# Scaling the near branch's probabilities on GpSimd instead of ScalarE in a sparse attention

## The chip, the core and the metric

The kernel runs on one core of a Trainium2 chip. Its engines work side by side, each on its own list of instructions in the order of the list, and they wait for each other through semaphores: TensorE (PE in the profile, its weight loads PEld), VectorE (DVE), ScalarE (ACT), GpSimd (POOL) and SyncE (SP), which issues DMAs. The metric is the time of one execution on the device in microseconds (us). A measurement here is the median of three executions.

## What is computed

The whole program is a block with two token mixers and an expert layer, followed by a context network of two layers. All is float32 with 256 tokens of 1024 features. The change is in the sparse attention of the first mixer, which is, cut to the part that matters:

```python
s_s = jnp.einsum('bgrtd,bgtmd->bgrtm', qb, ks) - slopes * dist_s      # selected blocks
p_s = masked_softmax(s_s, dist_s >= 0)
s_w = jnp.einsum('bgrtd,bgsd->bgrts', qb, kw) - slopes * dist_w       # the near (window) branch
p_w = masked_softmax(s_w, valid_w)
o_s = jnp.einsum('bgrtm,bgtmd->bgrtd', p_s, vs)
o_w = jnp.einsum('bgrts,bgsd->bgrtd', p_w, vw)
return gb[..., 0:1] * o_c + gb[..., 1:2] * o_s + gb[..., 2:3] * o_w
```

There are 8 heads of width 64 over 256 tokens. With 256 tokens the selected blocks and the window both span all keys, so each of the two branches is a 256 by 256 masked softmax per head, with its own keys and values, and both are mixed by gates. A third branch works on 15 compressed blocks.

## The kernel before

The program is a chain of stages. Long stages of matmuls, whose weights stream from memory and are split into a high and a low part (the lines L326, L332 and L705 to L707 that fill the profile), alternate with shorter ones that compute attentions and routings. Each stage is a block with one function for each engine, and a barrier stands between two blocks. The sparse attention is one block: it begins at 105.8 us of the profiled span, and the next block, the output projection `w_out`, starts its matmuls at 170.05 us. The HGRN recurrence (`hg`) and the compressed branch (`compare`) are woven into the same block.

The attention goes over 8 steps, (2 query blocks) x (4 pairs of heads), `NS = 8`. A step `u` works on 128 queries and two heads, and its scores lie as 2 halves (heads) of 512 columns: columns 0 to 255 are the selected branch, columns 256 to 511 the near branch. Each engine runs a loop over `i`, written by hand; in round `i` different engines are at different steps.

- TensorE, round i: the scores of step i (L1420, waits for the biased scores of step i-1), then the turning of the probabilities of step i-2 (L1429, 8 transposes of 128 by 128 from `pr` into PSUM), then what `hg` and `compare` put into this round, then the products with the values of step i-3 (L1450). Before the transposes stand two waits: `nsa_scaled` and `nsa_win_scaled` must both have reached u+1.
- VectorE, round i: the bias of step i (L1550, out of PSUM into `sc`) and its maximum (L1555), then `hg` and `compare`, then for step i-1 the chain that makes the scales: `sums` clipped (L1562), reciprocal (L1564), times the gates into `coef` (L1566), and then the selected columns of `pr` times `coef` (L1570, two instructions of 128x256). L1562, L1564 and L1566 each add one to `nsa_link`, so `nsa_link` of 3u+3 says that the scales of step u stand. L1570 adds to `nsa_scaled`.
- ScalarE, round i: copies of the turned probabilities of step i-2 from PSUM (L1600, `pT`), the four exponentials of step i with their sums (L1610, waits for the maximum), and then for step i-1 the near columns of `pr` times `coef` (L1616, two instructions of 128x256, after a wait for `nsa_link` of 3u+3), which adds to `nsa_win_scaled`.

`pr` has three buffers, `u % 3`. GpSimd does nothing in this block. In the block behind it, it adds up squares for a norm (L435, `tensor_tensor` of 128x256).

The two waits of TensorE, and what ScalarE does for them:

```python
pe.wait_ge(nsa_scaled, u + 1)
pe.wait_ge(nsa_win_scaled, u + 1)
...
act.wait_ge(nsa_link, 3 * u + 3)
for half in range(2):
    ins = act.activation(pr[:, u % 3, half, T:2 * T], pr[:, u % 3, half, T:2 * T], ACT.Copy, scale=coef[:, u % 3, 2 * half + 1:2 * half + 2])
ins.then_inc(nsa_win_scaled, 1)
```

Of the kernel before, what the change touches and what calls it, by code (L numbers as in the profile page):

```python
# [24 lines left out]
ACT = mybir.ActivationFunctionType  # L25
ALU = mybir.AluOpType
# [5 lines left out]
T = 256  # L32
# [150 lines left out]
def build(nc, dr):  # L183

    ctx = ExitStack()
    with ctx:
        def sem(name):
            return ctx.enter_context(nc.semaphore(name))
# [114 lines left out]
        def loads(sp, upto):  # L303

            for g in range(next_load[0], min(upto, n_pieces)):
                if g >= RAW:

                    _, _, split, n = pieces[g - RAW]
                    if g - RAW in own_end:
                        sp.wait_ge(*own_end[g - RAW])  # L310
                    else:
                        sp.wait_ge(lo_done if split else raw_used, n + 1)
                src, w, _, _ = pieces[g]
                sp.dma_start(raw[:, g % RAW, 0:w], src).then_inc(raw_loaded[g % RAW], 16)
            next_load[0] = max(next_load[0], min(upto, n_pieces))
# [4 lines left out]
        def split_hi(act, g):  # L320

            _, w, _, n = pieces[g]
            piece_loaded(act, g)
            if n >= SPLIT:
                act.wait_ge(piece_used, n - SPLIT + 1)
            act.activation(whi[:, n % SPLIT, 0:w], raw[:, g % RAW, 0:w], ACT.Copy).then_inc(hi_done, 1)  # L326
# [955 lines left out]
        NS = len(STEPS)  # L1282
        HALVES = [slice(0, 64), slice(64, 128)]
        nsa_scored, nsa_biased, nsa_max, nsa_exp = (sem(n) for n in ("nsa_scored_or_weighted_act", "nsa_biased_or_weighted_dve", "nsa_max_or_tokens_turned", "nsa_exp"))
        nsa_link, nsa_scaled, nsa_win_scaled = (sem(n) for n in ("nsa_link", "nsa_scaled", "nsa_win_scaled"))
# [7 lines left out]
        with ExitStack() as own, nc.Block() as block:  # L1293
            def ob(name, shape):
                return own.enter_context(nc.sbuf_tensor(name, shape, F32))
# [4 lines left out]
            pr = ob("nsa_pr", [P, 3, 2, 512])  # L1300
            nm, sums, coef = ob("nsa_nm", [P, 2, 4]), ob("nsa_sums", [P, 3, 4]), ob("nsa_coef", [P, 3, 4])
# [21 lines left out]
            def turn_bank(o):  # L1323
                return 2 + at_use[o] % 2
# [9 lines left out]
            @block.sync  # L1334
            def _(sp):
                loads(sp, at_wout + RAW)
# [244 lines left out]
            @block.scalar  # L1581
            def _(act):
                def block_done(qb):
                    bank = ps[:, 4 + qb, :]
                    act.wait_ge(block_attended, qb + 1)
                    act.activation(mixT[:, 4:8, qb * P:qb * P + P], bank.rearrange("p (c t) -> p c t", t=P), ACT.Copy).then_inc(block_out, 1)
                    act.activation(nsq[:, qb, :], bank, ACT.Square).then_inc(block_out, 1)

                def root(qb):
                    act.wait_ge(block_summed, qb + 1)  # L1590
                    act.activation(nroot[:, qb, :], ps[:, 4 + qb, 0:8], ACT.Sqrt, bias=eps[:, :], scale=1.0 / 64).then_inc(block_root, 1)

                for i in range(NS + 3):
                    if 0 <= i - 2 < NS:
                        u = i - 2
                        if u >= 2:
                            act.wait_ge(nsa_attended, u - 1)
                        for half in range(2):
                            act.wait_ge(nsa_turned, at_use[(u, half)] + 1)
                            act.activation(pT[:, u % 2, 512 * half:512 * half + 512], ps[:, turn_bank((u, half)), :], ACT.Copy).then_inc(nsa_copied, 1)  # L1600
                        if u == 2:
                            act.wait_ge(nsa_turned, at_use[("cmp", 0)] + 1)
                            act.activation(cT[:, :, :, :].rearrange("p h b t -> p (h b t)"), ps[:, turn_bank(("cmp", 0)), :], ACT.Copy).then_inc(nsa_copied, 1)
                    if i < NS:
                        act.wait_ge(nsa_max, i + 1)
                        if i >= 3:
                            act.wait_ge(nsa_turned, at_use[(i - 3, 1)] + 1)
                        for n in range(4):
                            half, a = divmod(n, 2)
                            act.activation(pr[:, i % 3, half, a * T:a * T + T], sc[:, i % 2, half, a * T:a * T + T], ACT.Exp, bias=nm[:, i % 2, n:n + 1],  # L1610
                                           accum_out=sums[:, i % 3, n:n + 1]).then_inc(nsa_exp, 1)
                    if 0 <= i - 1 < NS:
                        u = i - 1
                        act.wait_ge(nsa_link, 3 * u + 3)
                        for half in range(2):
                            ins = act.activation(pr[:, u % 3, half, T:2 * T], pr[:, u % 3, half, T:2 * T], ACT.Copy, scale=coef[:, u % 3, 2 * half + 1:2 * half + 2])  # L1616
                        ins.then_inc(nsa_win_scaled, 1)
                    if i == 2:
                        for b in range(TB):
                            act.wait_ge(hg_turned, b + 1)  # L1620
                            act.activation(kiT[:, b, :], ps[:, 6 + b, :], ACT.Copy).then_inc(hg_copied, 1)
                        act.wait_ge(cmp_link, 4)
                        act.activation(cs[:, :, :, :].rearrange("p h u n -> p (h u n)"), cs[:, :, :, :].rearrange("p h u n -> p (h u n)"), ACT.Exp).then_inc(cmp_exp, 1)
                    if i in (6, 7):
                        b = i - 6
                        act.wait_ge(hg_out, b + 1)
                        act.activation(osq[:, b, :], ps[:, 7 - b, :], ACT.Square).then_inc(hg_squared, 1)
                    if i == 7:
                        block_done(0)
                    if i == 8:  # L1630
                        act.wait_ge(hg_summed, 2)
                        act.activation(hsum[:, :, :], hsum[:, :, :], ACT.Sqrt, bias=eps[:, :], scale=1.0 / P).then_inc(hg_root, 1)
                    if i == 9:
                        root(0)
                block_done(1)
                root(1)

# [1623 lines left out]
```

## Time and profile before

| | |
|---|---|
| median of 3 runs | 2073.28 us (2072.81 to 2073.97) |
| the profiled execution | 2074.13 us |
| its span, first to last instruction | 2072.4 us |
| PE busy | 2004.6 us, 97% of the span |
| VectorE, ScalarE, GpSimd busy | 1458.1, 1063.0, 34.4 us |
| block of the sparse attention | about 105.8 to 169 us of the span |

Times in rows are us from the start of the span. A row of the timeline gives the start, the time until the end of the last of a run of like instructions, engine, line, operation, what is written and read, shape and count, and in brackets how long the engine had been idle before, with what ended it. "issue" there means that the profile shows nothing the engine waited for at that moment; a semaphore that came earlier, or a weight load, may stand behind it. In the table by stretches, PEclk is the mean granted clock of TensorE, 1.00 for 2.4 GHz and 0.50 for 1.2 GHz.

### The profile page before, as it was taken

Reading aid. Unit: us, or ns where it says so; the run is one execution under the profiler, and the core shown is the slowest. Engines: PE = TensorE matmul, PEld = TensorE weight load, DVE = VectorE, ACT = ScalarE, POOL = GpSimd, SP = SyncE. Lnnn points to the kernel's source line nnn. Section 1 sums busy time; section 2 is a strip of 40 time slices with the busy share of each in tenths; the row PEclk is TensorE's granted clock in tenths of the full one; section 3 lists DMA queues with packets and bytes.
Section 4 is the critical chain, followed back from the end, with each engine's and each line's share of the span. In section 5 each row is a group of like instructions: output and inputs, shape, how many; then the busy total and the mean of one; then the engine's idle time right before and its main releaser. Section 6 shows DMA issues by size and latency. Waiting matters only on the chain. (4 is left out here: it accounts for less than half of the span.)

```text
span 2072.4 us, 33517 instructions
## 1 busy us (share of the span) xinstructions
PE 2004.6 (97%) x13458; PEld 1765.5 (85%) x13458; DVE 1458.1 (70%) x2213; ACT 1063.0 (51%) x1979; POOL 34.4 (2%) x33
## 2 busy tenths in 40 slices
PE   8978999999999999999989999999999999999998
PEld 7858999999999888888787877878778888778998
DVE  7776599988888678888588657577774227667554
ACT  5674444467777555445573247453222227555444
POOL 0000000000000000000010000100000001000000
PEclk9988999999999999999999999999999999999999
DMA  6603566654444678777546520245674323125654
GB/s 224 206 1 122 164 191 185 192 168 139 143 133 143 198 245 267 250 257 259 162 135 200 171 67 22 92 133 173 232 272 136 100 94 98 42 69 157 194 188 127
DMA packets 95401, 328.98 MB, mean 159 GB/s; under 512 B 10384, under 2 KB 15888, under 8 KB 95248
## 3 DMA queue, kind: packets, MB, share of 16 engines
q1 hardware_dynamic: 95248, 326.85, 48.8%
q8 instruction: 107, 1.75, 0.3%
q14 instruction: 46, 0.38, 0.1%
HBM read 325.76 MB, written 1.05 MB: 158 GB/s over the span
## 5 line engine op out<-in xcount | busy, mean ns | idle before, releaser
L332 DVE TENSOR_TENSOR wlo<-raw,whi 128x1024 fp32r<-128x1024 f32 (+1 forms) x502 | 613.4, 1224 | 333.7 <-ACT whi L326 330.5
L326 ACT ACTIVATE whi<-raw 128x1024 fp32r<-128x1024 f32 (+1 forms) x502 | 525.5, 1049 | 380.9 <-PE ps L707 363.3
L705 PE MATMUL ps<-x_hi,whi 128*128 128x512 f32 (+1 forms) x976 | 333.5, 342 | 10.9 <-DVE x_lo L508 6.7
L706 PE MATMUL ps<-x_lo,whi 128*128 128x512 f32 (+1 forms) x976 | 329.9, 338 | 0.0
L707 PE MATMUL ps<-x_hi,wlo 128*128 128x512 f32 (+1 forms) x976 | 329.8, 338 | 0.0
L705 PE MATMUL ps<-xT_hi,whi 128*128 128x256 f32 x1136 | 324.1, 285 | 3.2 <-DVE xT_lo L506 2.8
L707 PE MATMUL ps<-xT_hi,wlo 128*128 128x256 f32 x1136 | 318.0, 280 | 0.0
L706 PE MATMUL ps<-xT_lo,whi 128*128 128x256 f32 x1136 | 317.9, 280 | 0.0
L705 PEld LDWEIGHTS ps<-x_hi,whi 128*128 128x128 f32 x976 | 184.1, 189 | 42.8 <-issue 13.6
L705 PEld LDWEIGHTS ps<-xT_hi,whi 128*128 128x128 f32 x1136 | 214.5, 189 | 3.5 <-issue 3.5
L706 PEld LDWEIGHTS ps<-xT_lo,whi 128*128 128x128 f32 x1136 | 214.5, 189 | 0.0
L707 PEld LDWEIGHTS ps<-xT_hi,wlo 128*128 128x128 f32 x1136 | 214.2, 189 | 0.0
L707 PEld LDWEIGHTS ps<-x_hi,wlo 128*128 128x128 f32 x976 | 184.3, 189 | 20.2
L706 PEld LDWEIGHTS ps<-x_lo,whi 128*128 128x128 f32 x976 | 184.3, 189 | 19.5 <-issue 0.2
L705 PE MATMUL ps<-whi,gh 128*128 128x512 f32 x512 | 200.1, 391 | 0.5 <-issue 0.5
L706 PE MATMUL ps<-wlo,gh 128*128 128x512 f32 x512 | 199.3, 389 | 0.0
L707 PE MATMUL ps<-whi,gl 128*128 128x512 f32 x512 | 199.3, 389 | 0.0
L1921 ACT ACTIVATE gh<-gated 128x256 fp32r<-128x256 f32 x128 | 53.4, 418 | 165.2 <-PE ps L707 165.2
L705 PE MATMUL ps<-ffn_hi,whi 128*128 128x512 f32 (+2 forms) x384 | 126.7, 330 | 0.9 <-DVE wlo L332 0.9
L707 PE MATMUL ps<-ffn_hi,wlo 128*128 128x512 f32 (+2 forms) x384 | 126.6, 330 | 0.0
L706 PE MATMUL ps<-ffn_lo,whi 128*128 128x512 f32 (+2 forms) x384 | 126.6, 330 | 0.0
L705 PEld LDWEIGHTS ps<-whi,gh 128*128 128x128 f32 x512 | 96.1, 188 | 22.6 <-issue 1.7
(431 smaller groups left out, 3331.8 us busy)
## 6 DMA issues: line engine op xcount, KB each, us to landing
raw<-peer_u_t SPq DMA_DIRECT2D x128, 512.0 KB, 3.6
raw<-peer_v_t SPq DMA_DIRECT2D x128, 512.0 KB, 4.0
raw<-ffn_in_t SPq DMA_DIRECT2D x88, 512.0 KB, 4.4
x<-ada_t SPq DMA_DIRECT2D x64, 512.0 KB, 4.5
raw<-ffn_out_t SPq DMA_DIRECT2D x44, 512.0 KB, 3.6
raw<-qkv_t SPq DMA_DIRECT2D x36, 512.0 KB, 4.2
gated<-ada_t SPq DMA_DIRECT2D x32, 512.0 KB, 5.9
raw<-w_in_t SPq DMA_DIRECT2D x24, 512.0 KB, 4.4
```

Source lines behind the costliest of these rows:

```text
L326: act.activation(whi[:, n % SPLIT, 0:w], raw[:, g % RAW, 0:w], ACT.Copy).then_inc(hi_done, 1)
L332: dve.tensor_tensor(wlo[:, n % SPLIT, 0:w], raw[:, g % RAW, 0:w], whi[:, n % SPLIT, 0:w].bitcast(F32), ALU.subtract).then_inc(lo_done, 1)
L705: pe.matmul(place, wh, xh, start=start, stop=False, skip_group_check=shared)
L706: pe.matmul(place, wh, xl, start=False, stop=False, skip_group_check=shared)
L707: return pe.matmul(place, wl, xh, start=False, stop=stop, skip_group_check=shared)
L1921: act.activation(gh[:, i % 3, :], gbuf[:, i, :], ACT.Copy).then_inc(gates_hi, 1)
```

## The change

The two ScalarE instructions at the end of each round are taken out, with their wait. GpSimd gets a function in this block: for each of the 8 steps it waits for the same `nsa_link` and multiplies the same columns with `tensor_scalar`, two instructions of 128x256, the second of which adds to `nsa_win_scaled`. TensorE and VectorE keep their instructions and waits.

```diff
                     if 0 <= i - 1 < NS:
                         u = i - 1
-                        act.wait_ge(nsa_link, 3 * u + 3)
-                        for half in range(2):
-                            ins = act.activation(pr[:, u % 3, half, T:2 * T], pr[:, u % 3, half, T:2 * T], ACT.Copy, scale=coef[:, u % 3, 2 * half + 1:2 * half + 2])
-                        ins.then_inc(nsa_win_scaled, 1)
+                        pass
...
+            @block.gpsimd
+            def _(pool):
+                for u in range(NS):
+                        pool.wait_ge(nsa_link, 3 * u + 3)
+                        for half in range(2):
+                            ins = pool.tensor_scalar(pr[:, u % 3, half, T:2 * T], pr[:, u % 3, half, T:2 * T], coef[:, u % 3, 2 * half + 1:2 * half + 2], None, ALU.mult)
+                        ins.then_inc(nsa_win_scaled, 1)
```

ScalarE's list in rounds 1 and 2 of the loop; `nsa_pr` are the probabilities, `nsa_coef` the scales, L1610 the exponentials, L1600 the copies of turned probabilities:

```order
 L1610 ACTIVATE nsa_pr,nsa_sums<-nsa_sc,nsa_nm 128x256 [waits nsa_max_or_tokens_turned]
 L1610 ACTIVATE nsa_pr,nsa_sums<-nsa_sc,nsa_nm 128x256 x3
-L1616 ACTIVATE nsa_pr<-nsa_pr,nsa_coef 128x256 [waits nsa_link]
-L1616 ACTIVATE nsa_pr<-nsa_pr,nsa_coef 128x256
 L1600 ACTIVATE nsa_pT<-ps 128x512 [waits nsa_turned] x2
```

Behind the exponentials of a step the copies of the step before now come at once; the wait for `nsa_link` is gone from ScalarE.

GpSimd's list at the start of the program and of the block; "ISA" is the instruction that the trace calls MODIFY_POOL_CONFIG:

```order
+L3254 MEMSET const-uint8-127 128x1
+L1635 UNCONDITIONAL_BRANCH [waits barrier_Pool_Activation_PE_DVE_SP_gather]
+L1640 ISA
+L1640 TENSOR_SCALAR nsa_pr<-nsa_pr,nsa_coef 128x256 [waits nsa_link]
+L1640 TENSOR_SCALAR nsa_pr<-nsa_pr,nsa_coef 128x256
```

The pair of L1640 stands there eight times. GpSimd's list where the next block begins, with the additions for the norm:

```order
+L1293 UNCONDITIONAL_BRANCH
 L844 UNCONDITIONAL_BRANCH [waits barrier_Pool_Activation_PE_DVE_SP_gather]
-L435 ISA
 L435 TENSOR_TENSOR x_ffn<-x_ffn 128x256 [waits early_squares]
 L435 TENSOR_TENSOR x_ffn<-x_ffn 128x256 [waits folded,early_squares] x3
```

The configuration has moved from the beginning of that block to the beginning of the attention's.

## Rows read from the trace of the kernel before

**Rows 1.** The page: span and busy time of the engines.

```profile
span 2072.4 us, 33517 instructions
...
PE 2004.6 (97%) x13458; PEld 1765.5 (85%) x13458; DVE 1458.1 (70%) x2213; ACT 1063.0 (51%) x1979; POOL 34.4 (2%) x33
```

**Rows 2.** One stretch: us long, busy by engine, PEclk, DMA share, GB/s.

```profile
150.00:160.00 10.00, 8.44 (x46) 7.81 (x47) 3.60 (x12) 7.70 (x18) 0.00 (x0) 0.54 0.00 0
```

**Rows 3.** Timeline of PE: the transposes of steps 0 to 4 and 6.

```profile
117.34 1.94 PE L1429 MATMUL ps<-kon,nsa_pr 128*128 128x128 f32 x8 [2.99 <-ACT nsa_pr L1616]
...
122.77 1.06 PE L1429 MATMUL ps<-kon,nsa_pr 128*128 128x128 f32 x8 [1.12 <-issue]
...
127.74 1.06 PE L1429 MATMUL ps<-kon,nsa_pr 128*128 128x128 f32 x8 [0.19 <-issue]
...
134.03 1.09 PE L1429 MATMUL ps<-kon,nsa_pr 128*128 128x128 f32 x8
...
139.69 1.06 PE L1429 MATMUL ps<-kon,nsa_pr 128*128 128x128 f32 x8 [0.73 <-issue]
...
151.56 1.94 PE L1429 MATMUL ps<-kon,nsa_pr 128*128 128x128 f32 x8 [3.55 <-issue]
```

**Rows 4.** Timeline of ACT: the near columns scaled, steps 0, 1, 2, 4, 6.

```profile
116.30 0.89 ACT L1616 ACTIVATE nsa_pr<-nsa_pr,nsa_coef 128x256 f32<-128x256 f32 x2
...
121.77 0.89 ACT L1616 ACTIVATE nsa_pr<-nsa_pr,nsa_coef 128x256 f32<-128x256 f32 x2
...
126.74 0.90 ACT L1616 ACTIVATE nsa_pr<-nsa_pr,nsa_coef 128x256 f32<-128x256 f32 x2
...
138.70 0.89 ACT L1616 ACTIVATE nsa_pr<-nsa_pr,nsa_coef 128x256 f32<-128x256 f32 x2
...
150.57 0.89 ACT L1616 ACTIVATE nsa_pr<-nsa_pr,nsa_coef 128x256 f32<-128x256 f32 x2
```

**Rows 5.** Timeline of DVE: the scales of steps 0 to 4, 6.

```profile
115.82 0.16 DVE L1566 TENSOR_TENSOR nsa_coef<-nsa_coef,gates 128x4 f32<-128x4 f32 x1
...
120.60 0.16 DVE L1566 TENSOR_TENSOR nsa_coef<-nsa_coef,gates 128x4 f32<-128x4 f32 x1
120.80 0.62 DVE L1570 TENSOR_SCALAR nsa_pr<-nsa_pr,nsa_coef 128x256 f32<-128x256 f32 x2
121.69 1.28 DVE L1550 SCALAR_TENSOR_TENSOR nsa_sc<-mkon,ps 128x512 f32<-128x512 f32 x2 [0.28 <-PE ps L1420]
...
126.47 0.17 DVE L1566 TENSOR_TENSOR nsa_coef<-nsa_coef,gates 128x4 f32<-128x4 f32 x1
...
132.30 0.16 DVE L1566 TENSOR_TENSOR nsa_coef<-nsa_coef,gates 128x4 f32<-128x4 f32 x1
...
138.04 0.16 DVE L1566 TENSOR_TENSOR nsa_coef<-nsa_coef,gates 128x4 f32<-128x4 f32 x1
...
149.47 0.17 DVE L1566 TENSOR_TENSOR nsa_coef<-nsa_coef,gates 128x4 f32<-128x4 f32 x1
```

**Rows 6.** PE and DVE where they wait for each other, 127 to 131 us.

```profile
130.88 1.13 PE L1367 MATMUL ps<-hg_v,sig 64*128 64x128 f32 x8 [1.11 <-DVE S L1478]
...
127.60 1.28 DVE L1550 SCALAR_TENSOR_TENSOR nsa_sc<-mkon,ps 128x512 f32<-128x512 f32 x2 [0.32 <-PE ps L1420]
```

**Rows 7.** GpSimd's line L435: ns shortest/median/longest, first and last start, forms.

```profile
L435 POOL TENSOR_TENSOR x<-x x24: 726/1292/2088, 1057.7 to 2063.9; 128x512 f32<-128x512 f32 x15, 128x256 f32<-128x256 f32 x9
L435 POOL TENSOR_TENSOR x_ffn<-x_ffn x4: 736/739/1587, 184.9 to 194.0; 128x256 f32<-128x256 f32 x4
L435 POOLq MODIFY_POOL_CONFIG  x2: 11/11/11, 169.0 to 169.0; - x2
```

**Rows 8.** Timeline, 2059 to 2066 us: GpSimd's additions beside DVE's tensor_scalar.

```profile
2060.21 2.51 POOL L435 TENSOR_TENSOR x<-x 128x256 f32<-128x256 f32 x3 [189.81 <-ACT x L425]
...
2061.11 0.88 DVE L2562 TENSOR_SCALAR final_weighted<-h,vec 128x256 f32<-128x256 f32 x1
...
2062.80 0.35 DVE L2562 TENSOR_SCALAR final_weighted<-h,vec 128x256 f32<-128x256 f32 x1
```

## The prediction

> **What bounds the kernel now.** I read the busy times first. TensorE is busy 2004.6 of the span's 2072.4 us, ScalarE half of it, GpSimd 2% [rows 1]. So nearly everywhere the time is matmuls, and an edit pays only where TensorE stands still. The block of the sparse attention is such a place: about 63 us in which all engines pass small pieces to one another. The blocks behind it are filled by matmuls without gaps, and nothing there has slack that depends on when it starts, so I carry a shift of this block's end one to one to the end of the program.
>
> Second, the timeline of TensorE within the block. Before the transposes (L1429) it stood idle for 2.99, 1.12, 0.19, 0.73 and 3.55 us at steps 0, 1, 2, 4 and 6, and not at all at step 3 [rows 3]. These are the places where the scaled probabilities came last; the row of step 0 names ScalarE's L1616.
>
> Third, who is late there. The scales of a step stand when VectorE's L1566 ends [rows 5]. From there to the end of ScalarE's two instructions [rows 4] it took: step 0, 117.19 less 115.98, 1.21 us; step 1, 122.66 less 120.76, 1.90; step 2, 127.64 less 126.64, 1.00; step 4, 139.59 less 138.20, 1.39; step 6, 151.46 less 149.64, 1.82. The two instructions themselves take 0.89 to 0.90 us; the rest is ScalarE still at the exponentials of the next step. TensorE starts 0.10 to 0.15 us after ScalarE's end (117.34, 122.77, 127.74, 139.69, 151.56) [rows 3]. So L1616 does end last at these five places, though VectorE's share (0.62 us for its own two [rows 5]) would be ready 0.3 to 1.2 us earlier.
>
> **What the change takes away.** ScalarE loses 16 instructions, 8 x 0.89 = 7.1 us of busy time. That is worth nothing by itself: ScalarE's exponentials wait for maxima or follow copies that wait for the transposes, so what it saves turns into waiting. The most that the change could bring is the near columns ready no later than VectorE's own: 0.04 + 0.62 us after the scales. Then TensorE would start earlier by 1.21 - 0.66 = 0.55 at step 0, 1.24 at step 1, 0.34 at step 2, 0.73 at step 4, 1.16 at step 6. These do not add up, because VectorE has its own chain. The gains of steps 0 to 2 end in TensorE's wait of 1.11 us for VectorE at 130.88, and VectorE itself can only close its own idle 0.28 and 0.32 us [rows 5, 6]: 0.6. Step 6 adds 1.16. That is the ceiling: about 1.8 us, under 0.1%.
>
> **What GpSimd costs.** The trace of before has no `tensor_scalar` on GpSimd. The nearest row is its `tensor_tensor` of the same 128x256: median 739 ns, 1587 at the longest [rows 7]. At 128x512 the median is 1292 ns, so 553 ns for 256 columns and 186 ns that do not depend on them. An instruction with one input instead of two might halve the 553: 186 + 277 = 0.46 us, my lower bound; 1.59 us is the upper. I take 0.74, the row of the same shape on the same engine.
>
> Then the port. VectorE's `tensor_scalar` of 128x256 takes 0.35 us alone, but 0.88 where it began while one of GpSimd's additions was running [rows 8], about as long as that addition's 0.74 and a little. So the two shut each other out. In the changed kernel they meet in every step: VectorE's L1570 and GpSimd's pair are released by the same semaphore. VectorE is a little ahead, since its own instruction set the semaphore. I let GpSimd wait for one of the two, 0.35 us. From the end of L1566 to GpSimd's end, which I call p: 0.1 for the semaphore + 0.35 + 2 x 0.74 = 1.93 us. Bounds: 0.1 + 2 x 0.46 = 1.0 without a wait, and 0.1 + 0.35 + 2 x 1.59 = 3.6.
>
> The Trainium skill (SBUF — State Buffer, section "Who interferes with whom") says that VectorE's `tensor_scalar` can enter a mode that takes the port pair it shares with GpSimd, and that the one that comes second waits for the whole instruction. The 0.88 above agrees. The skill's GPSIMD Engine Reference (section "When to use GPSIMD") speaks against the change in general: elementwise work belongs on VectorE, though one-input operations run at roughly line rate. By that rate p would be near its lower bound.
>
> **The sum, step by step.** GpSimd's end against ScalarE's end, each counted from the scales:
> - Step 0: 1.93 - 1.21 = +0.72. The transposes and what follows on TensorE, the scores for VectorE's L1550 at 121.69 included, come 0.7 later; VectorE was waiting for them (0.28 idle), so its whole list moves by 0.7.
> - Step 1: the scales come from VectorE's list before that, unmoved; 1.93 - 1.90 = +0.03.
> - Step 2: the scales are 0.7 late, and +0.93 on top: the transposes at +1.6. TensorE then has 1.11 us of waiting at 130.88 to give, so +0.5 is left; VectorE, with 0.32 idle at 127.60, is at +0.4 [rows 6]. Both go on at +0.5.
> - Step 3: TensorE came at 134.03 without a wait. The scales end at 132.46 + 0.5, GpSimd at 134.89, TensorE starts 0.15 later: 135.04, +1.0.
> - Step 4: the scales at +0.5, and 1.93 - 1.39 = +0.54: +1.0. TensorE itself is there at 1.0 - 0.73 = +0.3, so it waits for GpSimd.
> - From there TensorE works without a gap past step 5 to the scores of step 7, and VectorE follows them: the scales of step 6 at +1.0, and 1.93 - 1.82 = +0.11 more.
> - Behind step 6 TensorE is busy to the end of the attention, at half clock (151.56: the eight transposes take 1.94 us instead of 1.06 [rows 3]; mean granted clock 0.54 [rows 2]). Step 7's columns are ready before it gets to them.
>
> Sum: +1.1 us. The profiled execution took 2074.13 us, its span 2072.4 and 1.7 around it, so it would become 2075.2. The median of the runs is 0.85 below that execution; I forecast 2073.28 + 1.1 = 2074.4.
>
> GpSimd's other work costs nothing: its list in this block is otherwise empty, and the configuration that moved here is issued at about 105.9, ten us ahead of its first instruction, which waits for 115.98. No DMA moves, and SP's list is as before.
>
> **The rivals.** A measurement here can tell about 0.2% from no change, 4.1 us.
>
> 1. Cheap GpSimd: one input costs 0.46 us and the port does not bite, p = 1.0. Then step 0 is 0.2 early, step 1 0.9, step 2 unchanged, step 4 0.4 early, step 6 0.8; carried as above that leaves about 0.9 us gained: 2072.4. For it speaks the single input; against it the 0.88 of rows 8.
>
> 2. Dear GpSimd, the rival on the slower side: `tensor_scalar` with its scale read for each partition costs as much as the slowest rows of L435. At p = 3.6 the excess at step 0 is 2.4, at step 2 2.6, at step 4 2.2, at step 6 1.8, and TensorE's idle times (1.12, 1.11, 0.73) swallow only part: some 6.5 us, 2079.8. Between 0.74 (+1.1) and 1.59 (+6.5) it decides at 0.74 + 0.85 x 3.0 / 5.4, about 1.2 us for one instruction. Against it: the long rows of L435 stand beside two-input work on VectorE; alone it is 0.73 to 0.74 each time.
>
> 3. The configuration isn't hidden: something that follows MODIFY_POOL_CONFIG delays the first GpSimd instruction. Before, 15.9 us lay between it and the first addition (169.0 to 184.9), which took no longer than others [rows 7]; now 10.1 us lie there. The trace bounds a delay at 15.9 - 10.1 = 5.8 us, paid once, at step 0, and 4.5 after the idle times of steps 1 and 2: 2078.9 with the forecast's own 1.1.
>
> The Trainium skill (GPSIMD Engine Reference, section "Instruction dispatch") gives about 6 us for a first call after such a load; if that began only with the first call, it would be this rival, if it began with the configuration it would be hidden. No run here shows which.
>
> 4. The clock: TensorE fell to half clock after standing still for 2.99 and 3.55 us, not after 1.12 [rows 3]. With p = 1.93 it would stand for some 1.8 us before step 2. If that is enough, the groups after it take up to twice as long: 0.9 us for each set of eight transposes, some 1.8 us in all, 2076.2. Losing the low stretch behind 151.56 instead would gain 2 or 3 us, but the idle time before it does not get shorter.
>
> **How the numbers follow.** Forecast (p about 1.5 to 2.5) 0.62; cheap GpSimd 0.17; clock 0.08; dear GpSimd 0.08; configuration 0.05. Predicted 2074.4. The range goes down to the ceiling of the gain, 2073.28 - 1.8 = 2071.5, and up to where p is 2.9 or the clock falls once more, 2077.3; it leaves out most of rivals 2 and 3. Faster by over 0.2% would need more than twice the ceiling: 0.02. Slower by over 0.2%: rival 3 and most of rival 2, 0.11. The same: 0.87.
>
> **What would show it.** GpSimd's L1640 near 0.74 us each and its second one ending about 1.9 us behind L1566; VectorE's L1570 stretched from 0.62 towards 1.4 us where GpSimd got in between; TensorE's idle time before L1429 at step 2 grown from 0.2 to over 1 us; ScalarE 7 us less busy and waiting more; the next block's first matmul near 171.2 instead of 170.05. The forecast is wrong if L1640 takes over 1.2 us or under 0.5, if the first L1640 starts well after its semaphore, or if the low clock covers another stretch than before.

## The result

The changed kernel takes 2079.84 us (median of 20 runs, 2074.51 to 2082.09), the kernel before beside it 2074.74 us (20 runs, 2071.58 to 2076.50): the ratio is 1.0025 with a 95% interval of 1.0019 to 1.0031, 5.1 us slower. Forecast were 1.1 us. The profiled execution took 2079.41 us.

The page of the changed kernel, to be set beside [rows 1]: TensorE's busy time and GpSimd's have grown, ScalarE's has shrunk.

```profile
span 2077.6 us, 33517 instructions
...
PE 2008.0 (97%) x13458; PEld 1768.3 (85%) x13458; DVE 1460.0 (70%) x2213; ACT 1058.7 (51%) x1963; POOL 50.4 (2%) x49
```

The time went into the block of the sparse attention. In this profile the block's first scores began 0.69 us later than before (106.61 against 105.92 us; the mean clock over the program's first 50 us is 0.93 here and 1.00 there, and the change doesn't touch them), and the first matmul of the next block came at 175.33 instead of 170.05. So the block itself took 5.28 - 0.69 = 4.6 us longer, and all behind it as long as before (1904.1 us in both).

The timeline of the changed kernel's TensorE: the transposes of steps 0 to 4 and 6, which answer to [rows 3], and the scores of step 3.

```profile
119.60 1.94 PE L1429 MATMUL ps<-kon,nsa_pr 128*128 128x128 f32 x8 [3.87 <-POOL nsa_pr L1640]
...
123.18 2.08 PE L1420 MATMUL ps<-nqk 64*128 64x512 f32 x4
125.19 1.10 PE L1429 MATMUL ps<-kon,nsa_pr 128*128 128x128 f32 x8
...
132.42 1.94 PE L1429 MATMUL ps<-kon,nsa_pr 128*128 128x128 f32 x8 [2.41 <-issue]
...
138.51 1.09 PE L1429 MATMUL ps<-kon,nsa_pr 128*128 128x128 f32 x8
...
144.86 1.06 PE L1429 MATMUL ps<-kon,nsa_pr 128*128 128x128 f32 x8 [1.42 <-issue]
...
156.98 1.94 PE L1429 MATMUL ps<-kon,nsa_pr 128*128 128x128 f32 x8 [3.80 <-issue]
```

The brackets have grown: 3.87 instead of 2.99 at step 0, 2.41 instead of 0.19 at step 2. And there is something that no wait explains: at step 1 TensorE comes without a wait at 125.19, where it had waited 1.12 us before, because the eight transposes of step 0 and the groups behind them up to there ran at half clock. The scores of step 3 take 2.08 us here; the same ones took 1.13 in the kernel before.

The changed kernel's GpSimd at steps 0 and 2, and its VectorE beside it, to be set beside [rows 5]:

```profile
117.48 1.98 POOL L1640 TENSOR_SCALAR nsa_pr<-nsa_pr,nsa_coef 128x256 f32<-128x256 f32 x2 [117.05 <-DVE nsa_coef L1566]
...
130.33 1.99 POOL L1640 TENSOR_SCALAR nsa_pr<-nsa_pr,nsa_coef 128x256 f32<-128x256 f32 x2 [5.87 <-DVE nsa_coef L1566]
```

```profile
117.21 0.16 DVE L1566 TENSOR_TENSOR nsa_coef<-nsa_coef,gates 128x4 f32<-128x4 f32 x1
117.41 0.84 DVE L1570 TENSOR_SCALAR nsa_pr<-nsa_pr,nsa_coef 128x256 f32<-128x256 f32 x2
...
125.31 1.28 DVE L1550 SCALAR_TENSOR_TENSOR nsa_sc<-mkon,ps 128x512 f32<-128x512 f32 x2 [2.05 <-PE ps L1420]
...
130.07 0.17 DVE L1566 TENSOR_TENSOR nsa_coef<-nsa_coef,gates 128x4 f32<-128x4 f32 x1
```

From the end of L1566 (117.37) to the end of GpSimd's pair (119.46) it is 2.09 us; the forecast's p was 1.93. VectorE's pair takes 0.84 instead of 0.62. So the delay that the change puts in was sized about right, and yet VectorE's L1550 of step 3 starts 3.6 us later than before (125.31 against 121.69). Of these, 1.4 us were there when the scales of step 0 stood (117.37 against 115.98), before GpSimd's first instruction: 0.7 from the later start and 0.7 from the first groups of the block, which ran at a lower clock in this execution. From the scales of step 0 to L1550 it is 7.9 us instead of 5.7, 2.2 more, where I had 0.7.

Mean granted clock by stretches: PEclk is the number ahead of the last two. First the kernel before, the whole block, the part ahead of the first transposes and the part behind step 0:

```profile
105.70:168.80 63.10, 50.74 (x436) 40.33 (x436) 43.53 (x110) 39.66 (x111) 0.00 (x0) 0.86 0.00 1
105.70:117.00 11.30, 8.42 (x60) 5.77 (x60) 8.61 (x17) 6.04 (x19) 0.00 (x0) 0.83 0.00 0
117.00:127.00 10.00, 8.54 (x64) 6.88 (x64) 9.20 (x25) 8.47 (x27) 0.00 (x0) 0.85 0.01 2
```

The changed kernel, the whole block, the part ahead of the first transposes, the stretch from step 0 to step 1 and the one around steps 2 to 4:

```profile
106.40:174.10 67.70, 53.84 (x436) 42.13 (x436) 45.13 (x110) 33.57 (x95) 15.88 (x16) 0.80 0.00 1
106.40:119.60 13.20, 9.13 (x60) 6.26 (x61) 9.78 (x19) 5.45 (x17) 1.98 (x2) 0.76 0.00 0
119.60:126.00 6.40, 6.40 (x27) 4.57 (x28) 4.18 (x11) 4.53 (x14) 1.99 (x2) 0.56 0.00 0
...
132.40:145.00 12.60, 11.16 (x86) 8.42 (x87) 10.34 (x26) 6.92 (x21) 3.97 (x4) 0.88 0.00 1
```

The clock is lower over the block, 0.80 for 0.86, and the same 436 matmuls keep TensorE busy for 53.8 us instead of 50.7. These 3.1 us are two thirds of the block's 4.6; the other 1.5 us are standing (63.1 - 50.7 before, 67.7 - 53.8 now). 0.7 of the 3.1 us lie ahead of the first transposes (60 matmuls in 9.13 us for 8.42), where GpSimd had done nothing yet; the same slow beginning came in the profile of e4 below, where GpSimd is idle in the block, so I don't count it to the change. That leaves 3.9 us, 2.4 of slower matmuls and 1.5 of standing. The slow stretch that grew most lies at 119.6 to 126, where TensorE works without a gap (6.40 of 6.40 us) at little more than half clock; in the kernel before it was some 3 us long, behind step 0.

### The profile page after: what moved, and what is told of

It is laid out like the page before. It is cut to its first block and busy times, and to the rows that moved or that the text cites. A ratio compares the mean times of both kernels' runs of the same rounds, so it can differ in the third digit from the quotient of the medians.

```text
span 2077.6 us, 33517 instructions
## 1 busy us (share of the span) xinstructions
PE 2008.0 (97%) x13458; PEld 1768.3 (85%) x13458; DVE 1460.0 (70%) x2213; ACT 1058.7 (51%) x1963; POOL 50.4 (2%) x49
## 3 DMA queue, kind: packets, MB, share of 16 engines
HBM read 325.76 MB, written 1.05 MB: 157 GB/s over the span
```

## The theories and the experiments

**Clock theory:** GpSimd's lateness itself costs little. It makes TensorE stand longer before the transposes, the granted clock falls for longer, and TensorE then takes up to twice as long for the groups behind the wait. That is most of the 5 us. **Price theory**, the rival: the lateness is carried from step to step and is the whole loss; the clock is a bystander. **Port theory:** the collision with GpSimd, which stretches VectorE's pair, is what costs.

All twelve kernels had 5 to 11 runs with the kernel before beside them. "Behind" is the time from the end of L1566 until the last of the scaled columns stand, at step 0 of the profiled execution; block and clock are length and mean granted clock of the attention's block there. They are of one execution each. From the first scores to those of step 2, ahead of all that these kernels change, the blocks take between 7.3 and 8.2 us, with GpSimd at work and without it.

| kernel | behind, us | block, us | clock | median, us | before, us | ratio (95%) |
|---|---|---|---|---|---|---|
| before | 1.21 | 63.1 | 0.86 | 2074.74 | | |
| changed | 2.09 | 67.7 | 0.80 | 2079.84 | 2074.74 | 1.0025 (1.0019 to 1.0031) |
| e1_unscaled | | 60.9 | 0.85 | 2071.45 | 2073.43 | 0.9986 (0.9977 to 0.9995) |
| e2_pool_aside | | 60.3 | 0.88 | 2072.28 | 2073.43 | 0.9993 (0.9984 to 1.0002) |
| e3_after_filled | 2.1 | 60.9 | 0.97 | 2072.74 | 2073.43 | 0.9995 (0.9986 to 1.0004) |
| e4_before_filled | | 60.9 | 0.95 | 2072.57 | 2073.43 | 0.9994 (0.9985 to 1.0003) |
| e5_one_product | 1.5 | 66.6 | 0.81 | 2076.92 | 2074.20 | 1.0015 (1.0005 to 1.0024) |
| e6_half_each | 1.2 | 60.9 | 0.89 | 2071.92 | 2074.20 | 0.9994 (0.9985 to 1.0003) |
| e7_pool_behind | 2.6 | 70.0 | 0.79 | 2081.57 | 2074.20 | 1.0037 (1.0024 to 1.0051) |
| e8_vector_all | 1.2 | 60.2 | 0.90 | 2073.43 | 2074.20 | 0.9996 (0.9987 to 1.0005) |
| e11_fill_early | | 64.2 | 0.88 | 2075.70 | 2073.23 | 1.0006 (0.9997 to 1.0015) |
| e12_fill_late | | 64.2 | 0.87 | 2075.49 | 2073.23 | 1.0008 (0.9999 to 1.0017) |
| e9_vector_all_filled | | 60.2 | 0.96 | 2072.59 | 2073.23 | 0.9996 (0.9987 to 1.0005) |
| e10_half_each_filled | | 60.7 | 0.95 | 2071.64 | 2073.23 | 0.9994 (0.9985 to 1.0003) |

**What the wait is worth at most (e1).** From the changed kernel, GpSimd's function and TensorE's wait are taken out; the near columns stay unscaled.

```diff
-                        pe.wait_ge(nsa_win_scaled, u + 1)
...
-            @block.gpsimd
-            def _(pool):
-                ...
```

> The near columns are not multiplied by their scales at all, and TensorE waits only for VectorE's share; GpSimd is idle as before. It measures the most that any faster place for this work could bring. All theories: less than before. From the rows of before, TensorE would start 0.55, 1.24, 0.34, 0.73 and 1.16 us earlier at steps 0, 1, 2, 4 and 6, of which about 1.8 us reach the end: 1.8 us faster than before. The clock theory (the loss of the change is mostly TensorE's clock, which falls for longer where TensorE stands longer) adds that shorter standing makes less low clock: 2 to 4 us faster. The price theory (the loss is GpSimd's late end, carried through each step) says 1.8 and an unchanged clock.

It was 2.0 us faster than before by the medians, 1.0 to 4.8 by the interval, which agrees with the ceiling of 1.8. So by the medians no place for this work, however fast, could have gained more than 0.1%. The run doesn't tell the theories apart: 2.0 lies at the edge of the clock theory's 2 to 4, and the block's clock stayed as the price theory had it, 0.85 for 0.86.

**The port by itself (e2).** GpSimd does the same work into a buffer that nobody reads; TensorE doesn't wait for it and turns unscaled near columns; only ScalarE waits for it, before it overwrites a buffer that GpSimd still has to read.

```diff
-                        pe.wait_ge(nsa_win_scaled, u + 1)
...
+                            act.wait_ge(nsa_win_scaled, i - 2)
...
-                            ins = pool.tensor_scalar(pr[:, u % 3, half, T:2 * T], pr[:, u % 3, half, T:2 * T], ...
+                            ins = pool.tensor_scalar(aside[:, half, :], pr[:, u % 3, half, T:2 * T], ...
```

> GpSimd multiplies the near columns as in the changed kernel, beside VectorE's own pair, but into a buffer that nobody reads; TensorE does not wait for it and turns unscaled near columns. Only the collision on the port is left of the change. If the port is the cause (VectorE's second instruction stretched from 0.35 to 0.57 us in each of 8 steps): most of the loss stays, 3 us or more slower than before. If GpSimd's late end for TensorE is the cause, by its price or by the clock: within 0.5 us of the kernel without any scaling, so faster than before by 1 to 2 us.

1.1 us faster than before, 0.8 slower than e1 by the medians, with overlapping intervals. The port theory falls: with the collision in all eight steps and TensorE not waiting for GpSimd, the loss is gone.

**TensorE kept at work (e3, e4).** Both kernels get matmuls that nobody reads, where TensorE stands before the transposes. They write a bank that the transposes overwrite.

```diff
+                        if u in FILL:     # FILL = {0: 4, 1: 3, 2: 1, 4: 2, 6: 7}
+                            use((u, 0))
+                            for n in range(FILL[u]):
+                                pe.matmul(ps[:, turn_bank((u, 0)), 0:T], k("ident"), nqk[:, 4, :], start=True, stop=True)
                         pe.wait_ge(nsa_scaled, u + 1)
```

> The changed kernel, with matmuls added on TensorE that nobody reads, where it stands before the transposes of steps 0, 1, 2, 4 and 6 (4, 3, 1, 2 and 7 of 128x256). They keep it at work and fill waiting only. Clock theory: the low clock in this block goes, and the changed kernel comes down by 4 to 6 us, to 2074 or less, within 0.6 to 1.4 us of the kernel before with the same filling. Price theory: the gap to the kernel before with the same filling stays at 4 to 5 us.

> The kernel before with the same added matmuls. Clock theory: TensorE's low stretches at 117 to 120 and 151 to 161 us go, and it is 2 to 3.5 us faster than before; the changed kernel with this filling is 0.6 to 1.4 us slower than this one. Price theory: it is the same as before or a little slower by the filling, and 4 to 5 us faster than the changed kernel with the filling.

The changed kernel with the filling is 0.9995 of before, the kernel before with it 0.9994: the gap of 5.1 us has shrunk to 0.2 by the medians (each interval is about 2 us to either side). More instructions on TensorE have made the changed kernel some 6 us faster. The stretches of the two profiles, the changed kernel with the filling first:

```profile
106.30:167.20 60.90, 53.75 (x470) 40.84 (x470) 45.21 (x110) 33.03 (x95) 15.84 (x16) 0.97 0.00 1
```

```profile
107.10:168.00 60.90, 54.11 (x470) 41.64 (x470) 43.47 (x110) 39.29 (x111) 0.00 (x0) 0.95 0.00 1
```

Clock 0.97 and 0.95, and the same length of block. GpSimd is as late as ever: the timelines of GpSimd and TensorE at steps 0 and 2 of e3 show the pair of 1.98 us, and TensorE waiting for it, now 1.76 and 0.30 us after the filling, with transposes of 1.06 us:

```profile
116.72 1.97 POOL L1645 TENSOR_SCALAR nsa_pr<-nsa_pr,nsa_coef 128x256 f32<-128x256 f32 x2 [116.30 <-DVE nsa_coef L1571]
...
127.43 1.98 POOL L1645 TENSOR_SCALAR nsa_pr<-nsa_pr,nsa_coef 128x256 f32<-128x256 f32 x2 [3.74 <-DVE nsa_coef L1571]
```

```profile
118.84 1.06 PE L1434 MATMUL ps<-kon,nsa_pr 128*128 128x128 f32 x8 [1.76 <-POOL nsa_pr L1645]
...
129.51 1.06 PE L1434 MATMUL ps<-kon,nsa_pr 128*128 128x128 f32 x8 [0.30 <-issue]
```

The kernel before gained 0.9 us from the filling by the medians, not the 2 to 3.5 that I expected; its interval, 3.1 us faster to 0.6 slower, takes in most of these. In the profiles the stretch from the scores of step 2 to the next block's first matmul shows the filling without what lies ahead of it and behind it: 56.8 us before, 54.0 with the filling, which is 2.9 us less; 60.7 in the changed kernel, 54.4 with the filling. So the gap of 3.9 us between the two kernels becomes 0.5 there. The profiled executions as a whole are no measure of it: the one of e3 is the shortest of its eleven, the one of e4 the longest, and 3.1 of the 3.9 us between them lie behind the block.

**The filling in two parts (e11, e12).** The same, with `FILL = {0: 4, 1: 3}` and with `FILL = {6: 7}`.

> The changed kernel with the added matmuls at steps 0 and 1 alone (4 and 3). The runs so far: changed kernel 5.1 us over before, with all fillings 1 us under it. Clock theory: the low stretches at the beginning of the block (6.8 us at 118 to 125 and the 3.4 us at step 2 that followed in the changed kernel's profile) get shorter or go, the one of 10 us at the end stays: 1 to 4 us over before. Price theory, by which the filling worked in some other way than by the clock: either no effect (5 over) or all of it (1 under).

> The changed kernel with the added matmuls at step 6 alone (7), before the long low stretch at the end of the block. Clock theory: that stretch of 10 us, in which TensorE works without a gap at half clock, goes, and with it 2.5 to 4 us; the early stretches stay: 1 to 2.5 us over before, and the two partial fillings add up to about the whole. Price theory: as in the other partial filling.

2.5 and 2.3 us over before by the medians (the intervals reach down to no loss): each part takes back about half, where the price theory had nothing (5 us over before) or the whole (1 under), and each lifts the clock in its own place only. In the stretch from the scores of step 2 on, the parts add up to the whole: 60.7 us in the changed kernel, 57.9 and 57.2 with the parts, 54.4 with both. The kernel filled early, up to the last wait and behind it:

```profile
107.20:153.00 45.80, 37.77 (x314) 28.21 (x314) 36.93 (x83) 26.11 (x81) 12.54 (x13) 0.96 0.00 1
153.00:163.00 10.00, 8.55 (x47) 7.92 (x48) 3.77 (x11) 5.88 (x12) 3.33 (x4) 0.51 0.01 2
```

The kernel filled late, around steps 0 to 2 and behind:

```profile
118.00:133.00 15.00, 10.77 (x66) 7.71 (x67) 12.39 (x29) 7.58 (x23) 5.63 (x6) 0.75 0.00 1
133.00:170.80 37.80, 33.24 (x326) 26.92 (x324) 24.74 (x67) 20.32 (x55) 9.93 (x10) 0.95 0.00 1
```

The low stretch at the end of the block stood in the kernel before as well (0.54 in [rows 2]); filling it may repay time that the change had not cost. Of the low clock in the early part, some 3 us behind step 0 stood in the kernel before too; that it goes on to the scores of step 3, and that it returns at step 2, came with the change.

**More and less lateness (e7, e5, e6).** In e7 GpSimd waits for VectorE's pair; in e5 it does both halves in one `tensor_tensor`; in e6 it does one half and ScalarE the other.

```diff
-                        pool.wait_ge(nsa_link, 3 * u + 3)
+                        pool.wait_ge(nsa_scaled, u + 1)
```

> The changed kernel, but GpSimd waits until VectorE's own pair is done, so the two never meet on the port: VectorE's pair is back at 0.62 us, GpSimd starts 0.6 us later and its near columns stand about 2.6 us behind the scales instead of 2.1. If the collision were what costs, this is faster than the changed kernel. By the price theory it is about 0.5 to 1 us slower than the changed kernel, 6 us over before. By the clock theory the standing time at each step grows by 0.5 us, which may or may not tip the clock further: 5 to 9 us over before.

7.4 us over before. Without any collision GpSimd's pair takes 1.83 us, 0.92 for each:

```profile
118.19 1.83 POOL L1640 TENSOR_SCALAR nsa_pr<-nsa_pr,nsa_coef 128x256 f32<-128x256 f32 x2 [117.77 <-DVE nsa_pr L1570]
```

The columns stand 0.5 us later than in the changed kernel, and the whole takes 2 us more relative to before. Avoiding the collision doesn't help. The forecasts of both other theories (6 us, and 5 to 9) lie within the interval of 5.0 to 10.6 us, so the run doesn't tell them apart.

```diff
-                        for half in range(2):
-                            ins = pool.tensor_scalar(...)
+                        ins = pool.tensor_tensor(pr[:, u % 3, :, T:2 * T], pr[:, u % 3, :, T:2 * T],
+                                                 coef[:, u % 3, :].rearrange("p (h a) -> p h a", h=2)[:, :, 1:2].broadcast_to([P, 2, T]), ALU.mult)
```

> GpSimd multiplies both halves of the near columns in one tensor_tensor of 128x512, with the scales spread along the columns, instead of two tensor_scalar of 128x256. Its additions of 128x512 took 1.29 us in the kernel before (median), against 1.99 for the pair in the changed kernel, so the near columns should stand about 1.4 us behind the scales instead of 2.1. By the clock theory the standing time before the transposes of step 2 falls from 2.4 to about 1 us and the low stretch there goes: the kernel is within 1.5 us of before, some 4 us faster than the changed one. By the price theory, with the loss in proportion to the lateness, it is also near before (0 to +1). If the product is as dear as the pair (2 us), the loss stays at 5 us by both.

2.7 us over before: neither gone nor whole. GpSimd and VectorE at step 0 show why:

```profile
117.88 1.04 POOL L1639 TENSOR_TENSOR nsa_pr<-nsa_pr,nsa_coef 128x512 f32<-128x512 f32 x1 [117.44 <-DVE nsa_coef L1566]
```

```profile
117.83 1.50 DVE L1570 TENSOR_SCALAR nsa_pr<-nsa_pr,nsa_coef 128x256 f32<-128x256 f32 x2
```

GpSimd was faster than I thought, 1.04 us for both halves, but now VectorE is shut out for nearly all of it: its pair takes 1.50 us, and TensorE waits for VectorE. The columns stand 1.5 us behind the scales, the clock is 0.81. By the medians neither theory had this: both expected the kernel near before. The profiled execution, at 2079.5 us, is one of the longest of its eleven.

```diff
+                        pe.wait_ge(nsa_near_act, u + 1)
...
-                        pass
+                        act.wait_ge(nsa_link, 3 * u + 3)
+                        act.activation(pr[:, u % 3, 0, T:2 * T], pr[:, u % 3, 0, T:2 * T], ACT.Copy, scale=coef[:, u % 3, 1:2]).then_inc(nsa_near_act, 1)
...
-                        for half in range(2):
+                        for half in range(1, 2):
```

> GpSimd multiplies one of the two halves, ScalarE the other behind its exponentials as before. GpSimd's one instruction of 1.08 us ends 1.2 us behind the scales, ScalarE's one is 0.4 us earlier than its pair was. TensorE would start earlier by 0.0 to 0.4 us at the five steps than before: -0.5 us by the lateness alone, and by both theories between 2 us faster than before and the same. It tells whether half the load on GpSimd keeps any of the loss.

0.9994 of before, no loss, with GpSimd still in the block and still beside VectorE. Columns that stand 1.2, 1.5, 2.1 and 2.6 us behind the scales (e6, e5, the changed kernel, e7) go with 2.3 us faster than before (an interval that includes no change) and 2.7, 5.1 and 7.4 us slower by the medians: the later, the slower, and between 1.5 and 2.6 us nearly in proportion. The blocks of the profiles, 60.9, 66.6, 67.7 and 70.0 us at clocks of 0.89, 0.81, 0.80 and 0.79, look like a jump between 1.2 and 1.5, but they are one execution each, and in e5 VectorE is the late one. So these runs don't show by themselves whether the lateness works through the clock; e3 and e4 do.

**Candidates (e8, e9, e10).** VectorE does all four pieces; GpSimd's function and TensorE's wait for it are taken out. e9 is this kernel and e10 is e6, each with the full filling.

```diff
                             dve.tensor_scalar(pr[:, u % 3, half, 0:T], ..., coef[:, u % 3, 2 * half:2 * half + 1], None, ALU.mult)
+                            ins = dve.tensor_scalar(pr[:, u % 3, half, T:2 * T], pr[:, u % 3, half, T:2 * T], coef[:, u % 3, 2 * half + 1:2 * half + 2], None, ALU.mult)
```

> VectorE multiplies the near columns too: four tensor_scalar in a row instead of two, 0.27 us more for each, GpSimd idle, nothing on ScalarE. The near columns stand 1.2 us behind the scales, earlier than in the kernel before at steps 1, 4 and 6, the same at step 0, 0.2 later at step 2; VectorE's list gets 0.54 us longer in each of 8 steps, of which it has some to give where it waits for TensorE. Lateness alone: -0.9 to 0 us. Both theories: within 1.5 us of before.

> VectorE multiplies all four pieces, with the full filling on TensorE. A candidate for a faster kernel: VectorE's four pieces were 0.9 us faster than before, the filling 1.0. Clock theory: both together 1.5 to 2.5 us faster than before, since the low stretches are the same that both shorten. Price theory: 0.9 faster, as without the filling.

> One half on GpSimd and one on ScalarE, with the full filling. The other candidate: without the filling 1.2 to 1.7 us faster than before. With it 1.5 to 2.5 us faster by the clock theory, unchanged at 1.2 to 1.7 by the price theory.

0.9996, 0.9996 and 0.9994: all three medians lie 0.6 to 1.6 us under before, and each interval includes no change. None is shown to beat the kernel before; all beat the changed one. The clock theory's 1.5 to 2.5 us for e9 did not come, and e10's 1.6 fits the price theory's 1.2 to 1.7 as well. In the profiles the filling lifts the clock from 0.90 to 0.96 (e8 to e9) and from 0.89 to 0.95 (e6 to e10), and the block stays at 60.2 us and goes from 60.9 to 60.7. So in these two the higher clock gave the block nothing; what sets its length there, no run shows.

## Why the prediction was wrong

- **What bounds the block, and where ScalarE was late:** right. TensorE waited at the five places; e1 agrees with the ceiling of the gain, 1.8 us forecast and 2.0 measured (1.0 to 4.8).
- **GpSimd's price:** a little small. I took 0.74 us from the addition and 0.35 for the port; it is 0.92 us by itself (e7) and 1.08 and 0.92 beside VectorE, with 0.11 ahead of the pair, so p was 2.09 for 1.93. The estimate for one input, 0.46, was off by a factor of two: rival 1 is out. Rival 2 is out too: 1.08 us at the longest is under the 1.2 from which it was to decide.
- **The port:** who waits was wrong. GpSimd started 0.07 us behind VectorE and lost some 0.16 us; VectorE's second instruction lost the 0.22. It was worth little (e2, 0.8 us slower than e1 by the medians, with overlapping intervals).
- **The configuration:** hidden, rival 3 is out. The source view of the changed kernel has it at 106.6, and GpSimd's first instruction started at 117.48, 0.11 us behind the end of L1566:

```profile
L1640 POOL TENSOR_SCALAR nsa_pr<-nsa_pr,nsa_coef x16: 918/1000/1085, 117.5 to 158.7; 128x256 f32<-128x256 f32 x16
L1640 POOLq MODIFY_POOL_CONFIG  x2: 11/11/11, 106.6 to 106.6; - x2
```

  The 6 us that the Trainium skill (GPSIMD Engine Reference, section "Instruction dispatch") gives for a first call after a load did not appear 10.9 us behind the configuration; whether they are there and hidden, no run here shows.
- **The step that failed** is the sum's first, "Step 0: +0.72", with its follow-up "Step 1: +0.03". I added up delays with the groups on TensorE at the durations that they had before. The wait before step 0 did grow about as forecast, from 2.99 to 3.87 us. But the groups behind it up to step 3's scores ran at half clock, so from the scales of step 0 to VectorE's L1550 of step 3 it took 2.23 us longer instead of 0.7: 0.87 from the wait and 1.36 from the slower groups, for which the sum has no term. TensorE's idle 1.12 us before step 1, which would have swallowed some of it, was gone. At step 2 TensorE then stood for 2.41 us and fell again: its transposes at 132.42 took 1.94 us for 1.06, and the idle time behind them, 0.31 and 1.11 us before, was gone too; the sum had counted on the 1.11 ([rows 6]). In the profile the change cost 3.9 us of the block, 2.4 in slower matmuls and 1.5 in standing.
- **Rival 4** named that mechanism, at step 2 and with 1.8 us on top of the 1.1, and gave it 0.08. It missed step 0, where the clock already fell before the change: there was no new fall to look for, only a longer one. That the two effects feed each other (lower clock, later scores, later VectorE, longer standing) I did not carry. With the clock held up by the filling, the change costs 0.2 us by the medians and 0.5 in the profiles (e3 against e4), less than my 1.1 for the lateness.
- **The chance of slower by over 0.2%**, 0.11, was given to rivals 2 and 3, and it came by way of rival 4.

What stays open: how much of the 5.1 us the lateness would cost at a clock that never falls, 0.2 us or up to some 2 within the intervals. And the changed kernel's runs lie between 2074.5 and 2082.1 us, while one of them was profiled: its 4.6 us in the block, of which 3.9 come behind the slow beginning, are one case and not the mean.

## What to carry to other kernels

Where TensorE works in short groups between waits, price a longer wait by what the granted clock does behind it, not by the wait alone: read the clock and the duration of the same group in the rows before and behind each wait, and reckon that behind a wait that already drops the clock a longer wait can make the low stretch longer, as at step 0 here (some 3 us before, 5.6 in the changed kernel). Work that is moved off a busy engine is worth only what the engine that waits for it gains; here the ceiling, 1.8 us, could be read from the profile before anything was tried. And when such a block is slow, matmuls that nobody reads, placed where TensorE stands in both kernels, tell in two runs whether the difference comes by way of the clock: compare the two filled kernels with each other.

## What the runs showed of the hardware

- GpSimd's `tensor_scalar` of 128x256 with a scale for each partition took 0.92 us alone, more than its `tensor_tensor` of the same size (0.74, [rows 7]), and nearly as much as a `tensor_tensor` of 128x512 with the scales spread along the columns (1.04). One input was not cheaper than two.
- The two forms shut VectorE out differently. Beside GpSimd's `tensor_scalar`, VectorE's own pair of `tensor_scalar` went from 0.62 to 0.84 us; beside one `tensor_tensor` of 1.04 us it went to 1.50. The Trainium skill (SBUF — State Buffer, section "Who interferes with whom") has whoever issues first hold the shared ports for its whole instruction, while the other waits. In length the `tensor_tensor` agrees with that, though VectorE's instruction had started 0.05 us ahead of it (117.83 against 117.88); the `tensor_scalar` of 1.08 us, of which VectorE felt 0.22, does not.
- Behind the wait of 3.55 us at step 6 TensorE worked without a gap and still at half clock for most of 10 us (0.54 from 150 to 160 us in [rows 2], 0.51 from 153 to 163 us in e11). That isn't the same each time: in e6, behind 3.30 us, L1404 took 1.05 us again, 3.6 us after the transposes began; in the kernel before it took 1.87, 3.8 us after them.
- The wait ahead of a group doesn't tell by itself how fast the group runs. The transposes of step 2 took 1.94 us behind 2.41 us of standing in the changed kernel and 1.06 us behind 2.91 us in e7, where the low clock came one group later: L1367, from 134.89 on, took 2.07 us for 1.13.
